# Depthwise-convolution taps in a fused decoder kernel: a fourth channel block moves from VectorE to TensorE, and VectorE's four blocks are worked in pairs

## What is computed

```python
def conformer_conv(hn, w_in, b_in, w_dw, b_dw, ln_g, ln_b, w_out, b_out):
    a = hn @ w_in + b_in
    u, gate = jnp.split(a, 2, axis=-1)
    u = u * jax.nn.sigmoid(gate)
    u = lax.conv_general_dilated(u, w_dw[:, None, :], window_strides=(1,),
                                 padding=((CONV_WIDTH - 1, 0),),
                                 dimension_numbers=('NWC', 'WIO', 'NWC'),
                                 feature_group_count=D_MODEL) + b_dw
    u = jax.nn.silu(layer_norm(u, ln_g, ln_b))
    return u @ w_out + b_out

# of peer_ffn, for a chunk xc of 128 tokens and its chosen experts idx:
u = u_tab[idx]
act = jax.nn.gelu(jnp.einsum('td,thkd->thk', xc, u), approximate=False)
v = v_tab[idx]
return jnp.einsum('thk,thkd->td', (g * act).astype(v_tab.dtype), v)
```

## Time and profile before

| what | number |
|---|---|
| median of three runs | 1546.85 us |
| the profiled execution | 1552.11 us |
| its span (first to last instruction) | 1550.1 us |
| PE busy | 1038.0 us, 67% |
| VectorE busy | 1088.1 us, 70% |
| ScalarE busy | 616.1 us, 40% |
| GpSimd busy | 597.4 us, 39% |
| read from HBM | 608 MB, 393 GB/s over the span |
| chain that ended last | DMA 38%, PE 22%, DVE 21%, issue 12% |

### The profile page before, as it was taken

One profiled execution on the slowest core, in us unless ns is written; L12 is line 12 of the kernel. 1 busy time (PEld: TensorE's weight loads), 2 busy tenths in 40 slices (PEclk: granted clock), 3 DMA queues, 4 the chain that ended last, 5 costly groups with the idle time before them and its releaser, 6 DMA issues.

```text
span 1550.1 us, 20954 instructions
## 1 busy us (share of the span) xinstructions
PE 1038.0 (67%) x6788; PEld 525.2 (34%) x6788; DVE 1088.1 (70%) x2931; ACT 616.1 (40%) x1855; POOL 597.4 (39%) x516
## 2 busy tenths in 40 slices
PE   7998876777666678675866678576677644444543
PEld 3644442332334345332344355233244301101100
DVE  4446668777435779999655679599775676766784
ACT  2313446542233435555343435345434533333321
POOL 0014435453233445554333344244344344444441
PEclk9999887668778788776877789567788855556555
DMA  9549999999999999999999999999999999999996
GB/s 395 186 146 393 410 376 420 418 394 399 421 401 416 416 419 414 409 418 411 397 381 407 418 412 419 419 420 408 396 414 383 406 419 419 420 419 420 420 420 282
DMA packets 97145, 610.77 MB, mean 394 GB/s; under 512 B 11046, under 2 KB 18598, under 8 KB 28300
## 3 DMA queue, kind: packets, MB, share of 16 engines
q0 software_dynamic: 73728, 536.90, 84.5%
q1 hardware_dynamic: 22492, 72.28, 12.1%
q10 hardware_dynamic: 816, 0.25, 0.1%
HBM read 608.34 MB, written 1.05 MB: 393 GB/s over the span
## 4 chain that ended last, share of the span: by engine, by line
DMA 38%; PE 22%; DVE 21%; issue 12%; ACT 6%; POOL 2%; DVEq 0%; POOLq 0%; SPq 0%; ACTq 0%
DMA ring<-table_dram,idx 32%; PE bank L635 8%; DVE ring L1691 8%; PE ypsum L635 5%; PE qpsum L635 5%; DMA head<-heads_dram 3%; DVE arena L1579 2%; POOL ring L628 2%; ACT L1108 2%; PE spsum L635 1%; DMA arena<-heads_dram 1%; DMA arena<-c_out_dram 1%; ACT ring L1108 1%; DVE topi L1625 1%; ACT wts L1108 1%
## 5 line engine op out<-in xcount | busy, mean ns | idle before, releaser
L628 POOL DMA_INDIRECT ring<-table_dram,idx x512 | 597.2, 1166 | 930.5 <-PE ypsum L635 669.4
L1691 DVE CUSTOM_DVE_ANT_0 ring<-xns,ring 128x1024 f32<-128x1024 f32 x512 | 622.8, 1223 | 320.4 <-DMA ring<-table_dram,idx 316.4
L635 PE MATMUL ypsum<-ring,wts 128*32 128x256 f32 x4096 | 412.5, 498 | 430.0 <-ACT wts L1108 429.3
L1108 ACT ACTIVATE gel<-dot 128x1 f32<-128x1 f32 x512 | 103.0, 201 | 734.0 <-DVE dot L1691 732.9
L635 PEld LDWEIGHTS ypsum<-ring,wts 128*32 128x32 f32 x4096 | 99.5, 124 | 672.1 <-ACT wts L1108 613.8
L1108 ACT ACTIVATE wts<-gident,gel 128x32 f32<-128x32 f32 x512 | 164.6, 321 | 17.0 <-ACT gel L1108 0.2
L635 PE MATMUL qpsum<-head,hT 128*128 128x256 f32 (+1 forms) x324 | 97.9, 464 | 26.6 <-DMA head<-heads_dram 23.1
L1108 ACT ACT_TABLE_LOAD x84 | 107.8, 1283 | 8.3 <-PE bank L640 6.8
L1579 DVE SCALAR_TENSOR_TENSOR arena<-arena,cols 128x128 f32<-128x128 f32 x300 | 88.4, 346 | 0.7
L635 PEld LDWEIGHTS qpsum<-head,hT 128*128 128x128 f32 (+1 forms) x324 | 71.1, 226 | 49.1 <-issue 19.3
L635 PE MATMUL qpsum<-arena 128*128 128x128 f32 x372 | 83.7, 361 | 0.0
(11 more groups left out here) (191 smaller groups left out, 1011.4 us busy)
## 6 DMA issues: line engine op xcount, KB each, us to landing
head<-heads_dram SPq DMA_DIRECT2D x28, 512.0 KB, 8.9
arena<-heads_dram SPq DMA_DIRECT2D x34, 256.0 KB, 7.1
ring<-table_dram,idx POOLq DMA_INDIRECT x512, 12.6
arena<-c_in_dram SPq DMA_DIRECT2D x4, 2048.0 KB, 16.3
arena<-heads_dram SPq DMA_DIRECT2D x7, 1152.0 KB, 25.3
ring<-w_in_dram SPq DMA_DIRECT2D x3, 2048.0 KB, 18.6
arena<-c_out_dram SPq DMA_DIRECT2D x6, 1024.0 KB, 7.9
arena<-w_out_dram SPq DMA_DIRECT2D x1, 4096.0 KB, 37.6
```

What stands on the lines that cost most here:

```text
L628: pool.indirect_dma_start(out=row(b), out_offset=None, in_=table[:, :], in_offset=bass.IndirectOffsetOnAxis(ap=idx[R % 2][:, k:k + 1], axi ...
L635: return nc.tensor.matmul(o_, l, r, start=start, stop=stop, **kw)
L1108: return nc.scalar.activation(out_, in_, func, **kw)
L1691: V.tensor_tensor_reduce(out=u, in0=xnr[G % 2], in1=u, scale=1.0, scalar=0.0, op0=ALU.mult, op1=ALU.add, accum_out=dot[:, k:k + 1]).then_i ...
```

## The change

Block 4 goes from VectorE's list to TensorE's. VectorE keeps blocks 0 to 3, in two pairs, 124 taps over slots 17 to 77 (two in nearly every slot, in place of two or three). TensorE has 124 taps over slots 21 to 74: two in a slot, and three in slots 24, 27, 31, 34, 37, 41 and so on up to 74 (16 of 54). `GLU_ORDER` is set so that each block's product is there in time, and the wait of a VectorE tap is one instruction back throughout. DIAGS stays at 4.

```diff
-GLU_ORDER = [0, 1, 2, 6, 7, 5, 3, 4]
+GLU_ORDER = [0, 1, 6, 7, 5, 2, 3, 4]
 GLU_SLOT = [6 + 4 * i for i in range(KD)]
-TAPS_FROM, TAPS_TO = 21, 78
-DVE_TAPS = [(c, k) for some in ((0, 1, 2), (3, 4)) for k in range(TAPS) for c in some]
-PE_TAPS = [(c, k) for c in (6, 7, 5) for k in range(TAPS)]
-PE_TAPS_FROM, PE_TAPS_TO = 29, 75
+TAPS_FROM, TAPS_TO = 17, 78
+DVE_TAPS = [(c, k) for two in ((0, 1), (2, 3)) for k in range(TAPS) for c in two]
+PE_TAPS = [(c, k) for c in (6, 7, 5, 4) for k in range(TAPS)]
+PE_TAPS_FROM, PE_TAPS_TO = 21, 75
 DIAGS = 4
@@ in VectorE's tap @@
-                own.wait(2 if c < 3 else 1)
+                own.wait(1)
```

## The result

The changed kernel takes **1558.69 us** (median of 6 runs, 1556.79 to 1561.9) against 1546.87 for before (6 runs on the same chip): a ratio of 1.0072, 95% interval 1.0058 to 1.0086. That is 11 us slower. The forecast said 1548.3 and a range that ended at 1553.5. The sign of its sum and the place of the loss were right; the size was not.

What follows compares the result with a forecast made beforehand. The prediction took nearly full DMA engines as the bound, 2.50 us a slot. Its terms, 1.0 + 2.1 - 1.65 = +1.45 us, carried over to the median of 1546.85, gave 1548.3 us, range 1543 to 1553.5.

Steps and rivals of the forecast that it cites:

- The bound: Whole kernel: DMA engines almost full, a slot cannot cost less than 2.50 us; ceiling of any gain 4 us.
- VectorE's relief: Slots 68 to 72: fewer VectorE taps make the two late dips shallower, -0.75 and -0.9, together -1.65 us.
- dips at 704 and 1079: Short drops in DMA rate at 704 and 1079 us, 379 and 353 GB/s, losing 0.95 and 1.9 us.
- Linked slots: Slots 24, 25, 27, 28, 31 and so on: a diagonal needs TensorE's first tap of the same slot; 0.75 us idle each.
- The walk: Slots 25 to 37, first convolution, step by step: `add_slot` 28 comes 3.7 us later, `add_slot` 37 8.9 us later.
- It frees the buffer of slot 44 ... 2.1 us late: `add_slot` 37 at 615.0 frees slot 44's buffer; its gather lands at 622.1 against 620.05 due, 2.1 us late.
- The 2.1 replaces the dip at 623: First convolution: 2.1 us of lateness takes the place of the DMA dip at 623 us (1.07), net +1.0 us.
- From slot 38 on ... lateness shrinks: After the last `glu` half a linked slot takes 2.0 us, below 2.50, so lateness shrinks.
- The two convolutions: Lateness costs +1.0 us in the first, +2.1 in the second; VectorE gains 0.75 and 0.9 at the late dips.
- The links' term: Waits from linked slots beside `glu` halves: +1.0 us in the first convolution, +2.1 in the second.
- The slower rival, links at half clock: TensorE's pauses between 570 and 610 us bring its clock down: 7.8 us, about 1554 to 1556; chance 0.20.
- Against it: TensorE has more work there: Argument against the half-clock rival: TensorE has more work in the tap stretches than before; no size of its own.

Runs made afterwards that it cites:

- with filler: The changed kernel plus 24 matmuls of 128 x 128, sums thrown away, in TensorE's pauses ahead of `add_slot`: 1553.72 us against 1547.1, ratio 1.0046.

## Why the prediction was wrong in size

- *The bound.* Nothing contradicts it: with no link beside a `glu` half every version that was run lies within 1.5 us of before, below the 4 us that were called the ceiling.
- *VectorE's relief, -1.65 us.* Its signs came (240 taps, and with five buffers shallower dips at 704 and 1079). The change with five buffers measures it together with the added work: -1.1 us, with an interval from -2.9 to +0.8.
- *Linked slots.* Right, and shown by five runs. The walk said that `add_slot` 28 comes 3.7 us later and `add_slot` 37 8.9. From slot 20, which starts 3.8 us earlier in the profile of after, they came 3.5 (585.85 for 586.20) and 11.8 us later (614.08 for 606.12); with filler, at the full clock, 37 came 10.0 later.
- *"It frees the buffer of slot 44 ... 2.1 us late": this is the step that failed.* `add_slot` 37 was 2.9 us later than the walk said, and the gather of slot 44 landed 6.4 us after its issue, where the shortest of the earlier trace rows, 5.6, had been taken. 2.1 + 2.9 + 0.8 = 5.8. It landed at 622.0 (615.56 + 6.4), 5.7 us behind a pace of 2.50 from 556.25. Of the 2.9, filler took away 1.8 (11.8 to 10.0): that is the half clock, which the walk left to a rival. The other 1.1 is not traced further. The arithmetic was right; its inputs, every `glu` half at full clock and the shortest landing, were the best case.
- *"The 2.1 replaces the dip at 623."* No run shows that anything was replaced: from slot 48 to slot 51 the lateness rose from 6.4 to 7.4 us in the changed kernel and stayed at 6.2 in the filled one. Whether the old dip is a part of this rise was not tried.
- *"From slot 38 on ... lateness shrinks."* True of `add_slot`: 11.8 us at slot 37, 5.6 at slot 41 (623.27 for 621.43). But the rows that were late stayed late, 7.4 us at slot 51 and 8.0 at slot 79: the DMA engines moved 419 GB/s from 641 to 711 us, what they move without a convolution, and so had no speed left to make it up.
- *The two convolutions.* They were to lose 1.0 - 0.75 = 0.25 us and 2.1 - 0.9 = 1.2, and by the table lost 4.9 and 6.0. The links' term, 1.0 + 2.1 = 3.1 us in the sum, measured about 12: 8 at the full clock and 4 for the half clock.
- *The slower rival, links at half clock.* Its condition came about exactly: the halves of slots 28 and 34 in the first convolution, and of slot 28 in the second. "Against it: TensorE has more work there" was the weak argument: the links cut that work into bursts with pauses. Its price was 7.8 us; 4 was measured, with about 3 either way, and it came on top of a base that was too low.

In all: -1 us for relief and work, +8 for the links, +4 for the clock, 11 us. These are differences of the same few ratios, so that they add up is no proof of them.

## What to carry to other kernels

When a step is made to pass more items through a small buffer between two engines, count for each item which slot of the consumer frees its place; if it is the slot that the producer is still feeding, both queues run in step. Here one more buffer (0.9993) and keeping such slots away from the consumer's long work (0.9993) each gave all of it back. Price a late transfer with a landing time from such a stretch, not with the shortest of the whole run, and where the DMA engines are nearly full, as here, do not count on a late row being made up. Judge waits by where they lie: 82 us of them cost nothing in one version, and 11 us of time went with 92 in another.

## What was not expected of the hardware

- A gather's landing time shrinks less than the prediction took when fewer are under way. Line 628 between 584 and 613 us, the time from issue to landing, in the changed kernel:

```profile
DMA to landing us min/median/max: 6.5/7.4/7.6
```

  In before it was 8.6, 11.1 and 12.9 there. From 10 gathers issued in these 29 us after and 13 before, an estimate is 10 x 7.4/29 = 2.6 under way at a time against 13 x 11.1/29 = 5.0. So half as many under way still took 7.4 us each in the median, three slots' worth of time.
- TensorE's granted clock fell from 1.00 to 0.50 (1.2 GHz) within 1 us after the pauses of 1.68 us ahead of slot 28 and 1.18 us ahead of slot 34, and came back after 3 to 4 us of work. The same pause of 1.18 us ahead of slot 34 in the second convolution was not followed by a fall: that half (963.38 us) took 2.05 us. Nor were longer ones, 1.90 and 1.78 us ahead of slots 22 and 24 in the first (565.26 and 572.10 us, 2.05 each). With filler the pauses ahead of slots 25 to 38 were 0.80 us or less, and every half from slot 26 on took 2.05 us.
